# Two-layer mLSTM / sparse-attention trunk: seven block products per gate-and-up pair in both layers, with the first pair's splits in another order

## The chip, the cores and the metric

The kernel is one program on one core of a Trainium2 chip. The metric is device time in microseconds (us), the median of several executions; less is better. TensorE (PE) does the matrix products, VectorE (DVE), ScalarE (ACT) and GpSimd (POOL) the elementwise work, and SyncE (SP) issues the loads of weights.

## The reference, cut to what matters

Activations are 512 tokens by 1024 features in fp32, and the model has two layers. Each layer is a mixer (mLSTM and differential attention in layer 0, sparse attention in layer 1) and a gated feed-forward part:

```
def swiglu_ffn(h, norm_g, w_gate, w_up, w_down):
    y = rmsnorm(h, norm_g)
    return (jax.nn.silu(y @ w_gate) * (y @ w_up)) @ w_down

for layer in range(DEPTH):
    y = rmsnorm(h, mix_norms[layer])
    if layer % 2 == 0:
        h = h + mlstm_diff_mixer(y, pos, layer, *mix_params[layer])
    else:
        h = h + nsa_mixer(y, pos, *mix_params[layer])
    h = h + swiglu_ffn(h, *ffn_params[layer])
return rmsnorm(h, final_norm)
```

`w_gate` and `w_up` are 1024 x 2816, `w_down` is 2816 x 1024. The change touches `y @ w_gate` and `y @ w_up` alone.

## The kernel before, in words

**Split operands.** Every large product is made of fp32r operands in two parts, high and low: high x high, high x low, low x high, three matmuls that add up in one PSUM bank. ACT copies a weight tile to its high part (`split_high`), DVE subtracts to get the low part (`split_low`), PE multiplies.

**Units.** Weights come in units of 1024 x 128, one load each. A table (`UNIT_LIST`) numbers them through the whole program. A raw unit goes to slot number mod `RAW` (4), its split to slot number mod `SPL` (2). SP issues the load of unit u once the low split of unit u - 4 is done. Each engine runs its own instructions in the order in which they are written; semaphores alone tie the engines together.

**Gate and up stage.** It has 22 pairs (`HT`), a gate unit and an up unit each. A plain unit is 24 matmuls of 128 x 512 (`feature_unit`, 8 tiles of the inner dimension by 3). After it DVE takes the bank, times the norm's factor `rinv`, into a `work` tile (`take`); when both halves of a pair are taken and ACT has made the silu, POOL multiplies them (`product`), ACT makes the high part of the result (`ffn_high`) and DVE the low (`ffn_low`).

**Fast pairs.** `FAST` is `(1,)`: in layer 1 the first 6 pairs (`PLAIN`) are plain and the other 16 are done by `fast_quad`. The pair's weights are a 2 x 2 array of blocks (A11, A12 the halves of the gate unit, A21, A22 those of the up unit), y is another (B11 to B22: halves of the features by halves of the tokens), and seven block products stand in for eight, on sums of blocks: A11 x B11, A12 x B21, S2 x T2, S1 x T1, S3 x T3, S4 x B22, A22 x T4. Each is 12 matmuls of 128 x 256, so a pair is 84 of these where a plain pair is 48 of 128 x 512. Between them ACT copies partial results out of PSUM (`fast_copy`), and the next product into that bank waits for the copy (`part_taken`). The y blocks, scaled by `rinv` beforehand (`y_scaled`), their sums (`y_sum`) and their splits (`y_form_high`, `y_form_low`; tiles high_B, high_T, low_B, low_T) are made by DVE and ACT while the plain units run. For each pair DVE makes sums of weight blocks (`first_sums`, `second_sums`) and ACT and DVE split them: `gate_form_*` for A11 and A12, `s13_*` for S1 and S3, `s24_*` for S2 and S4 (both in the tile s_s_forms: of the program before, line 1837 and line 2546 are s13, line 1846 and line 2552 are s24), `a22_*` for A22 (tile a_high, a_low). The space of s_s_forms is that of the plain units' splits, so that the first s13 and s24 must wait for the last plain unit. The sums and T2 to T4 lie over the residual `hT` and over the constants, so ACT sends the residual to DRAM when the stage begins (`residual_spill`) and fetches it when the stage ends.

**Layer 0** does its 22 pairs plainly, from loops (`Fori`).

Of the kernel before, what the change touches and what calls it, by code (L numbers as in the profile page):

```python
# [82 lines left out]
def run(name, count, first=0):  # L83
# [9 lines left out]
UNIT_LIST = (L0_UNITS + run("WO0", 8) + run("UP0", 2 * HT) + run("DN0", 16) + L1_UNITS  # L93
             + run("WO1", 8) + run("UP1", 2 * HT) + run("DN1", 16))
# [12 lines left out]
FAST = (1,)  # L107
PLAIN = 6
NFAST = HT - PLAIN
FAST_UNITS = {AT[f"UP{layer}", c] for layer in FAST for c in range(2 * PLAIN, 2 * HT)}  # L110
FORMS = ("A11", "A12", "S2", "S1", "S3", "S4", "A22")
# [304 lines left out]
def trunk(nc, A, consts, out):  # L416
    with ExitStack() as ctx:
# [444 lines left out]
        def _(pe):  # L862
# [2313 lines left out]
```

## Time and profile before

| | us |
|---|---|
| median of 3 runs | 1317.62 (1317.62 to 1317.81) |
| the profiled execution, its own time | 1319.15 |
| its span in the trace | 1317.4 |
| PE busy | 1301.3 (99% of the span) |
| DVE busy | 782.5 (59%) |
| ACT busy | 605.6 (46%) |
| POOL busy | 195.6 (15%) |

What lies around the span is 1.75 us in the profiled execution. The granted TensorE clock was 1.00 of full speed nearly throughout. A plain unit's matmuls and a fast pair's are told apart by their width, 128x512 and 128x256.

### The profile page before, as it was taken

To read this page: it belongs to the slowest core of one execution; us is meant where nothing else is said; L and a number is where in the kernel's file an instruction comes from. 1 tells how busy PE (TensorE), PEld (TensorE's weight loads), DVE (VectorE), ACT (ScalarE), POOL (GpSimd) and SP (SyncE) were. 2 spreads that over 40 slices of the span, in tenths; PEclk is the share of its full clock that TensorE was granted. 3 is DMA by queue.
4 is the path that set the end of the run, shared out by engine and by line. 5 is a ranking of instruction groups with operands and counts; after the bars stand their busy time and mean duration, and the time that the engine had idled before them with its cause. 6 is when DMAs were issued, how large, how long until landed. Compare 5 with 4: busy or idle time off the path is not lost.

```text
span 1317.4 us, 18990 instructions
## 1 busy us (share of the span) xinstructions
PE 1301.3 (99%) x6992; PEld 1069.3 (81%) x6992; DVE 782.5 (59%) x1407; ACT 605.6 (46%) x1111; POOL 195.6 (15%) x212
## 2 busy tenths in 40 slices
PE   9999999999999999999999999999999999999997
PEld 7777788888888888888888875568887999998887
DVE  5678886543333333323599778776476788873222
ACT  4435765433333332222285457785434566652222
POOL 2003571221111110110000002112211000010100
PEclk9999999999999999999999999999999899999999
DMA  8332222323333333332244310001432333445311
GB/s 251 82 80 65 64 65 65 97 85 99 99 99 97 96 106 111 93 105 65 83 117 136 103 33 16 2 1 33 145 108 68 97 97 99 123 127 170 109 45 64
DMA packets 206728, 118.53 MB, mean 90 GB/s; under 512 B 5792, under 2 KB 203680, under 8 KB 206272
## 3 DMA queue, kind: packets, MB, share of 16 engines
q1 hardware_dynamic: 205936, 113.03, 29.8%
q10 hardware_dynamic: 304, 4.20, 0.8%
q0 software_dynamic: 416, 0.35, 0.3%
q8 instruction: 44, 0.72, 0.2%
q14 instruction: 28, 0.23, 0.1%
HBM read 113.37 MB, written 4.19 MB: 89 GB/s over the span
## 4 chain that ended last, share of the span: by engine, by line
PE 90%; DVE 3%; ACT 2%; POOL 2%; issue 2%; DMA 0%; SPq 0%; POOLq 0%; DVEq 0%; ACTq 0%
PE acc L865 17%; PE acc L867 17%; PE acc L866 17%; PE acc L1185 4%; PE acc L1187 4%; PE acc L1188 4%; PE acc L1516 3%; PE acc L878 2%; PE acc L879 2%; PE acc L882 2%; PE aux L1503 2%; PE aux L1423 2%; PE acc L919 1%; PE acc L1423 1%; PE acc L920 1%
## 5 line engine op out<-in xcount | busy, mean ns | idle before, releaser
L715 DVE TENSOR_TENSOR w_low<-raw_units,w_high 128x1024 fp32r<-128x1024 f32 (+2 forms) x152 | 200.9, 1322 | 362.0 <-ACT w_high L696 361.9
L696 ACT ACTIVATE w_high<-raw_units 128x1024 fp32r<-128x1024 f32 (+2 forms) x153 | 170.7, 1116 | 260.4 <-PE acc L867 222.4
L865 PE MATMUL acc<-y_high,w_high 128*128 128x512 f32 x616 | 244.6, 397 | 1.5 <-DVE w_low L715 1.5
L867 PE MATMUL acc<-y_high,w_low 128*128 128x512 f32 x616 | 240.3, 390 | 0.0
L866 PE MATMUL acc<-y_low,w_high 128*128 128x512 f32 x616 | 239.9, 389 | 0.0
L865 PE MATMUL acc<-ffn_high,w_high 128*128 128x512 f32 (+1 forms) x374 | 141.0, 377 | 0.0
L866 PE MATMUL acc<-ffn_low,w_high 128*128 128x512 f32 (+1 forms) x374 | 140.8, 377 | 0.0
L867 PE MATMUL acc<-ffn_high,w_low 128*128 128x512 f32 (+1 forms) x374 | 140.8, 377 | 0.0
L865 PEld LDWEIGHTS acc<-y_high,w_high 128*128 128x128 f32 x616 | 115.2, 187 | 26.9 <-DVE w_low L715 2.4
L867 PEld LDWEIGHTS acc<-y_high,w_low 128*128 128x128 f32 x616 | 115.1, 187 | 25.4
L866 PEld LDWEIGHTS acc<-y_low,w_high 128*128 128x128 f32 x616 | 115.3, 187 | 23.9 <-issue 0.5
L867 PEld LDWEIGHTS acc<-ffn_high,w_low 128*128 128x128 f32 x374 | 70.4, 188 | 13.0
L865 PEld LDWEIGHTS acc<-ffn_high,w_high 128*128 128x128 f32 x374 | 70.4, 188 | 12.8
L866 PEld LDWEIGHTS acc<-ffn_low,w_high 128*128 128x128 f32 x374 | 70.4, 188 | 12.8
L3034 POOL TENSOR_TENSOR work<-work,work 128x512 f32<-128x512 f32 x28 | 39.8, 1422 | 260.4 <-DVE work L2154 260.4
L2080 ACT ACTIVATE score<-score,neg_max 128x384 f32<-128x384 f32 (+3 forms) x128 | 68.7, 540 | 18.7 <-DVE neg_max L2898 18.5
L3020 POOL TENSOR_TENSOR work<-work,work 128x512 f32<-128x512 f32 x31 | 42.1, 1357 | 225.2 <-ACT work L1609 224.8
L1792 ACT ACTIVATE ffn_high<-work 128x512 f32 (+1 forms) x28 | 17.7, 633 | 101.0 <-POOL work L3034 101.0
L1185 PE MATMUL acc<-high_T,s_s_forms 128*128 128x256 f32 x192 | 55.7, 290 | 3.8 <-DVE s_s_forms L2552 3.8
L1187 PE MATMUL acc<-low_T,s_s_forms 128*128 128x256 f32 x192 | 55.5, 289 | 0.0
L1188 PE MATMUL acc<-high_T,s_s_forms 128*128 128x256 f32 x192 | 55.5, 289 | 0.0
L2154 DVE TENSOR_TENSOR work<-acc,rinv 128x512 f32<-128x512 f32 x64 | 43.8, 685 | 13.2 <-ACT rinv L1613 7.2
(410 smaller groups left out, 2662.3 us busy)
## 6 DMA issues: line engine op xcount, KB each, us to landing
raw_units<-in_l_w_gate_dram SPq DMA_DIRECT2D x44, 512.0 KB, 3.9
raw_units<-in_l_w_up_dram SPq DMA_DIRECT2D x44, 512.0 KB, 3.9
raw_units<-in_l_w_down_dram SPq DMA_DIRECT2D x32, 704.0 KB, 4.6
raw_units<-in_l_w_in_dram SPq DMA_DIRECT2D x43, 512.0 KB, 3.9
raw_units<-in_l_w_out_dram SPq DMA_DIRECT2D x16, 512.0 KB, 4.1
raw_units<-in_l_w_in_dram SPq DMA_DIRECT2D x10, 256.0 KB, 3.1
raw_units<-in_l_cmp_w_k_dram SPq DMA_DIRECT2D x4, 512.0 KB, 3.9
raw_units<-in_l_cmp_w_v_dram SPq DMA_DIRECT2D x4, 512.0 KB, 4.2
```

The costliest lines, as they stand in the source:

```text
L696: act.activation(dst, src, ACT.Copy).then_inc(S("split_high"), 1)
L715: dve.tensor_tensor(dst, src, high.bitcast(F32), ALU.subtract).then_inc(S("split_low"), 1)
L865: pe.matmul(o, ah, bh, start=first, stop=False)
L866: pe.matmul(o, ah, bl, start=False, stop=False)
L867: return pe.matmul(o, al, bh, start=False, stop=last)
L1185: pe.matmul(out, wh_k, y_high_of[y][:, c], start=start and k == 0, stop=False, skip_group_check=True)
L1187: pe.matmul(out, wh_k, y_low_of[y][:, c], start=False, stop=False, skip_group_check=True)
L1188: mm = pe.matmul(out, wl_k, y_high_of[y][:, c], start=False, stop=(k == KT // 2 - 1), skip_group_check=True)
L2080: act.activation(probs_at(n), probs_at(n), ACT.Exp, scale=-1.0, bias=nmx[:, n % 16:n % 16 + 1], accum_out=rsum[:, n % 16:n % 16 + 1]).then ...
L2154: return dve.tensor_tensor(dst, ps(tile)[lo:hi, cols], rinv[lo:hi, cols], ALU.mult)
L3020: pool.tensor_tensor(tmp[0][:, 0:T], tmp[0][:, 0:T], tmp[1 + m % 2][:, 0:T], ALU.add)\
L3034: pool.tensor_tensor(up, tmp[2 * (t % 2)][:, 0:T], up, ALU.mult).then_inc(S("ffn_prod"), 1)
```

## The change

`FAST` becomes `(0, 1)`: layer 0's last 16 pairs are done by seven products too, with places of their own for its y. A unit that is never loaded (`GAP0`, `GAP1`) stands ahead of the fast pairs in the numbering, so that a pair lies in an even and the next odd raw slot. The constants from `K_ROPEC` on, which layer 0's forms overwrite, are fetched again by ACT's queue behind the residual. In both layers s24 is made ahead of s13 for every pair, and PE waits for each by itself; ahead of the first fast pair ACT makes the gate form and s24, s13 before the ffn_high of the same step, DVE the sums and the gate form before it takes unit 10, and the y forms lie one step apart (T4 at step 9).

```
-FAST = (1,)
+FAST = (0, 1)
 PLAIN = 6
 NFAST = HT - PLAIN
+def up_units(layer, first):
+    gap = run(f"GAP{layer}", (first + 2 * PLAIN) % 2)
+    return run(f"UP{layer}", 2 * PLAIN) + gap + run(f"UP{layer}", 2 * NFAST, 2 * PLAIN)
...
             def load(eng, u, view, src, it=0, per=0):
+            last = u - RAW if u - RAW not in GAPS else u - 2 * RAW
+            if last in FAST_UNITS:
+                name, c = stage_of(last)
+                eng.wait_ge(S("form_low"), forms_split(int(name[2]), c // 2) + (2 if c % 2 else 4))
...
@@ fast_quad, on PE @@
-                pe.wait_ge(S("form_low"), forms_split(layer, t) + 3)
+                pe.wait_ge(S("form_low"), forms_split(layer, t) + 2)
                 pe.wait_ge(S("part_taken"), 4 * q + 1)
                 product("S2", "T2", x)
-                pe.wait_ge(S("form_low"), forms_split(layer, t) + 2)
+                pe.wait_ge(S("form_low"), forms_split(layer, t) + 3)
                 product("S1", "T1", z)
...
@@ fast_up, on ACT @@
-                hi_at = {3: ["B11"], 4: ["B21"], 5: ["T1", "B22"], 6: ["T2"], 7: ["T3"], 8: ["T4"]}
+                hi_at = {3: ["B11"], 4: ["B21"], 5: ["T1"], 6: ["B22"], 7: ["T2"], 8: ["T3"], 9: ["T4"]}
...
-                    ffn_post(layer, c // 2, c % 2)
+                    if c == 2 * PLAIN - 2:
+                        gate_form_high(layer, PLAIN)
+                    if c == 2 * PLAIN - 1:
+                        s24_high(layer, PLAIN)
+                        s13_high(layer, PLAIN)
                     for f in hi_at.get(c, ()):
                         y_form_high(layer, f)
-                    if c == 2 * PLAIN - 2:
-                        gate_form_high(layer, PLAIN)
-                s13_high(layer, PLAIN)
-                s24_high(layer, PLAIN)
+                    ffn_post(layer, c // 2, c % 2)
...
                 act.dma_start(hT, spill).then_inc(S("residual_moved"), 16)
+                if layer == 0:
+                    act.dma_start(kc[:, K_ROPEC:K_END], consts[:, K_ROPEC:K_END]).then_inc(S("consts_in"), 16)
...
@@ fast_up, on DVE @@
-                low_at = {4: ["B11"], 5: ["B21"], 6: ["T1", "B22"], 7: ["T2"], 8: ["T3", "T4"]}
+                low_at = {4: ["B11"], 5: ["B21"], 6: ["T1", "B22"], 7: ["T2"], 8: ["T3"], 9: ["T4"]}
...
+                    if c == 2 * PLAIN - 2:
+                        first_sums(layer, PLAIN)
+                        gate_form_low(layer, PLAIN)
+                        second_sums(layer, PLAIN)
                     ffn_post(layer, c // 2, c % 2)
...
-                    if c == 2 * PLAIN - 2:
-                        first_sums(layer, PLAIN)
-                        gate_form_low(layer, PLAIN)
-                        second_sums(layer, PLAIN)
+                s24_low(layer, PLAIN)
                 s13_low(layer, PLAIN)
-                s24_low(layer, PLAIN)
```

On ACT, from the split of unit 10 in layer 1 to the first copy of the first fast pair, before (w_high is a unit's split, `work_62<-work_62` a silu):

```order
L696 ACTIVATE w_high_56<-raw_units 128x1024
L1787 ACTIVATE work_60<-work_60 128x512
L1816 ACTIVATE high_T_134<-y_t_170 128x1024
L696 ACTIVATE w_high_58<-raw_units 128x1024
L1792 ACTIVATE ffn_high<-work_61 128x512
L1787 ACTIVATE work_62<-work_62 128x512
L1828 ACTIVATE gate_form_high<-raw_units 128x1024
L1792 ACTIVATE ffn_high<-work_63 128x512
L1837 ACTIVATE s_s_forms<-s_s_sums_149 128x2x512
L1846 ACTIVATE s_s_forms<-raw_units 128x2x512
L1855 ACTIVATE a_high<-raw_units 128x512
L1871 ACTIVATE work_60<-acc 128x256
```

and of the changed kernel (line 1862 is s24, line 1853 is s13), the same stretch, which stands alike in layer 0:

```order
L711 ACTIVATE w_high_58<-raw_units 128x1024
L1832 ACTIVATE high_T_133<-y_scaled_first 128x1024
L1803 ACTIVATE work_60<-work_60 128x512
L711 ACTIVATE w_high_56<-raw_units 128x1024
L1832 ACTIVATE high_T_134<-y_t_191 128x1024
L1808 ACTIVATE ffn_high<-work_61 128x512
L1844 ACTIVATE gate_form_high<-raw_units 128x1024
L1803 ACTIVATE work_62<-work_62 128x512
L1862 ACTIVATE s_s_forms<-raw_units 128x2x512
L1853 ACTIVATE s_s_forms<-s_s_sums_148 128x2x512
L1808 ACTIVATE ffn_high<-work_63 128x512
L1871 ACTIVATE a_high<-raw_units 128x512
```

The two splits into s_s_forms have moved ahead of the last plain pair's ffn_high, and s24 is the first of them; the copy of the first partial result still stands behind that ffn_high.

On DVE, from the split of unit 11 in layer 1, before:

```order
L715 TENSOR_TENSOR w_low_59<-raw_units,w_high_58 128x1024
L2154 TENSOR_TENSOR work_61<-acc,rinv 128x512
L2154 TENSOR_TENSOR work_62<-acc,rinv 128x512
L2461 TENSOR_TENSOR ffn_low<-work_61,ffn_high 128x512
L2530 TENSOR_TENSOR s_s_sums_149<-raw_units 128x2x512
L2519 TENSOR_TENSOR gate_form_low<-raw_units,gate_form_high 128x1024
L2539 TENSOR_TENSOR raw_units<-s_s_sums_149,raw_units 128x512
L2541 TENSOR_TENSOR raw_units<-raw_units 128x512
L2154 TENSOR_TENSOR work_63<-acc,rinv 128x512
L2546 TENSOR_TENSOR s_s_forms<-s_s_sums_149,s_s_forms 128x2x512
L2552 TENSOR_TENSOR s_s_forms<-raw_units,s_s_forms 128x2x512
```

and of the changed kernel:

```order
L2173 TENSOR_TENSOR work_61<-acc,rinv 128x512
L2529 TENSOR_TENSOR low_T_141<-y_t_191,high_T_134 128x1024
L2550 TENSOR_TENSOR s_s_sums_148<-raw_units 128x2x512
L2539 TENSOR_TENSOR gate_form_low<-raw_units,gate_form_high 128x1024
L2559 TENSOR_TENSOR raw_units<-s_s_sums_148,raw_units 128x512
L2561 TENSOR_TENSOR raw_units<-raw_units 128x512
L2173 TENSOR_TENSOR work_62<-acc,rinv 128x512
L2481 TENSOR_TENSOR ffn_low<-work_61,ffn_high 128x512
L2173 TENSOR_TENSOR work_63<-acc,rinv 128x512
L2572 TENSOR_TENSOR s_s_forms<-raw_units,s_s_forms 128x2x512
L2566 TENSOR_TENSOR s_s_forms<-s_s_sums_148,s_s_forms 128x2x512
```

The sums and the gate form have moved ahead of the take of unit 10 (work_62), so that they no longer stand between it and the take of unit 11 (work_63).

## Rows read from the trace of the kernel before

**Rows 1.** The page's busy times (us, share of the span, instructions), PE alone

```profile
PE 1301.3 (99%) x6992; PEld 1069.3 (81%) x6992; DVE 782.5 (59%) x1407; ACT 605.6 (46%) x1111; POOL 195.6 (15%) x212
```

**Rows 2.** The chain that ended last, shares by engine

```profile
PE 90%; DVE 3%; ACT 2%; POOL 2%; issue 2%; DMA 0%; SPq 0%; POOLq 0%; DVEq 0%; ACTq 0%
```

**Rows 3.** Busy times by stretch: layer 0, its down stage, layer 1

```profile
core 0: us, PE busy (x) PEld busy (x) DVE busy (x) ACT busy (x) POOL busy (x), PEclk, DMA share, GB/s
268.21:509.43 241.22, 241.22 (x1068) 199.53 (x1066) 95.04 (x112) 77.00 (x91) 30.46 (x24) 1.00 0.34 98
509.43:629.11 119.68, 119.68 (x530) 99.13 (x528) 36.38 (x32) 31.11 (x31) 11.34 (x9) 1.00 0.32 93
947.16:1016.43 69.27, 67.75 (x300) 55.18 (x298) 49.19 (x53) 28.13 (x34) 13.31 (x8) 1.00 0.38 115
1016.43:1033.13 16.70, 12.87 (x85) 12.67 (x84) 9.87 (x13) 7.42 (x11) 2.03 (x2) 0.80 0.23 64
1033.13:1184.33 151.20, 151.20 (x1262) 151.20 (x1261) 126.19 (x162) 92.26 (x148) 12.31 (x15) 1.00 0.40 110
```

**Rows 4.** Timeline of PE in layer 1: start, duration, idle before and its releaser

```profile
992.97 0.50 PE L865 MATMUL acc<-y_high,w_high 128*128 128x512 f32 x1 [0.26 <-DVE w_low L715]
...
1005.41 0.50 PE L865 MATMUL acc<-y_high,w_high 128*128 128x512 f32 x1 [1.25 <-DVE w_low L715]
...
1016.20 0.39 PE L867 MATMUL acc<-y_high,w_low 128*128 128x512 f32 x1
...
1019.18 0.28 PE L1188 MATMUL acc<-high_B,gate_form_low 128*128 128x256 f32 x1
1023.29 0.58 PE L1185 MATMUL acc<-high_T,s_s_forms 128*128 128x256 f32 x1 [3.83 <-DVE s_s_forms L2552]
...
1029.00 0.35 PE L1188 MATMUL acc<-high_T,s_s_forms 128*128 128x256 f32 x1
```

**Rows 5.** Timeline of ACT, around units 10 and 12, and one later pair

```profile
1001.57 0.63 ACT L1792 ACTIVATE ffn_high<-work 128x512 fp32r<-128x512 f32 x1 [5.49 <-POOL work L3034]
1002.11 1.04 ACT L1816 ACTIVATE high_T<-y_scaled_first 128x1024 fp32r<-128x1024 f32 x1
1003.06 1.04 ACT L696 ACTIVATE w_high<-raw_units 128x1024 fp32r<-128x1024 f32 x1
...
1019.27 0.63 ACT L1792 ACTIVATE ffn_high<-work 128x512 fp32r<-128x512 f32 x1 [5.12 <-POOL work L3034]
1019.80 1.04 ACT L1837 ACTIVATE s_s_forms<-s_s_sums 128x1024 fp32r<-128x1024 f32 x1
...
1021.69 0.61 ACT L1855 ACTIVATE a_high<-raw_units 128x512 fp32r<-128x512 f32 x1
1022.21 0.36 ACT L1871 ACTIVATE work<-acc 128x256 f32<-128x256 f32 x1
...
1044.85 0.38 ACT L1871 ACTIVATE work<-acc 128x256 f32<-128x256 f32 x1 [0.81 <-PE acc L1188]
```

**Rows 6.** Timeline of DVE from the take of unit 11

```profile
1017.12 0.68 DVE L2154 TENSOR_TENSOR work<-acc,rinv 128x512 f32<-128x512 f32 x1
1020.87 1.23 DVE L2546 TENSOR_TENSOR s_s_forms<-s_s_sums,s_s_forms 128x1024 fp32r<-128x1024 f32 x1 [3.08 <-ACT s_s_forms L1837]
1022.02 1.22 DVE L2552 TENSOR_TENSOR s_s_forms<-raw_units,s_s_forms 128x1024 fp32r<-128x1024 f32 x1
```

**Rows 7.** Timeline of POOL: products of the plain pairs 3 and 5

```profile
998.26 3.28 POOL L3034 TENSOR_TENSOR work<-work,work 128x512 f32<-128x512 f32 x1 [10.12 <-DVE work L2154]
...
1017.94 1.29 POOL L3034 TENSOR_TENSOR work<-work,work 128x512 f32<-128x512 f32 x1 [5.93 <-DVE work L2154]
```

**Rows 8.** DMA issues: size and median us to landing

```profile
raw_units<-in_l_w_gate_dram SPq DMA_DIRECT2D x44, 512.0 KB, 3.9
...
residual<-residual_spill ACTq DMA_DIRECT2D x1, 2048.0 KB, 9.3
...
shape_constants<-shape_consts_dram SPq DMA_DIRECT2D x1, 1480.0 KB, 10.5
```

More of the change, by code:

```diff
@@ L92 @@
             + run("VSW", 4))
-UNIT_LIST = (L0_UNITS + run("WO0", 8) + run("UP0", 2 * HT) + run("DN0", 16) + L1_UNITS
-             + run("WO1", 8) + run("UP1", 2 * HT) + run("DN1", 16))
+FAST = (0, 1)
+PLAIN = 6
+NFAST = HT - PLAIN
+def up_units(layer, first):
+    gap = run(f"GAP{layer}", (first + 2 * PLAIN) % 2)
+    return run(f"UP{layer}", 2 * PLAIN) + gap + run(f"UP{layer}", 2 * NFAST, 2 * PLAIN)
+UNIT_LIST = L0_UNITS + run("WO0", 8)
+UNIT_LIST += up_units(0, len(UNIT_LIST)) + run("DN0", 16) + L1_UNITS + run("WO1", 8)
+UNIT_LIST += up_units(1, len(UNIT_LIST)) + run("DN1", 16)
 UNITS = len(UNIT_LIST)
@@ L104, in stage_of @@
     return UNIT_LIST[u]
-FAST = (1,)
-PLAIN = 6
-NFAST = HT - PLAIN
 FAST_UNITS = {AT[f"UP{layer}", c] for layer in FAST for c in range(2 * PLAIN, 2 * HT)}
+GAPS = {u for u, (name, _) in enumerate(UNIT_LIST) if name[:3] == "GAP"}
 FORMS = ("A11", "A12", "S2", "S1", "S3", "S4", "A22")
@@ L115, in split_count @@
 def split_count(u):
-    return u + 1 - sum(f <= u for f in FAST_UNITS)
+    return u + 1 - sum(f <= u for f in FAST_UNITS | GAPS)
 def unit_count(u):
@@ L155, in loads_of @@
 def loads_of(u):
-    return 2 if stage_of(u)[0] == "VSW" else 1
+    return 0 if u in GAPS else 2 if stage_of(u)[0] == "VSW" else 1
 def loads_in_slot(u):
@@ L534, in trunk @@
                             .rearrange("p (f w) -> p f w", f=2)[:, :, 0:T])
-        plain_y = {3: ([row(f"y3_high{m}", 28 + m, 1, F32R) for m in range(KT)],
+        plain_y = {1: ([row(f"y1_high{m}", 8 + m, 1, F32R) for m in range(KT)],
+                       [row(f"y1_low{m}", 28 + m, 1, F32R) for m in range(KT)]),
+                   3: ([row(f"y3_high{m}", 28 + m, 1, F32R) for m in range(KT)],
                        [row(f"y3_low{m}", r, 1, F32R) for m, r in enumerate((36, 37, 38, 39, 40, 41, 6, 7))])}
-        scaled = {3: [row("y3_scaled_first", 8, 4), row("y3_scaled_last", 12, 4)]}
-        t_raw = {3: {"T1": row("y3_t1", 16, 2), "T2": row("y3_t2", 18, 2), "T4": row("y3_t4", 16, 2)}}
+        scaled = {1: [row("y1_scaled_first", 16, 4), row("y1_scaled_last", 36, 4)],
+                  3: [row("y3_scaled_first", 8, 4), row("y3_scaled_last", 12, 4)]}
+        t_raw = {1: {"T1": row("y1_t1", 40, 2), "T2": row("y1_t2", 6, 2), "T4": row("y1_t4", 40, 2)},
+                 3: {"T1": row("y3_t1", 16, 2), "T2": row("y3_t2", 18, 2), "T4": row("y3_t4", 16, 2)}}
         qraw = row("q_raw", 0, 8)
@@ L811, in load_ffn @@
                         w = (w_gate if c % 2 == (c >= 2 * PLAIN) else w_up)[layer]
-                        tile = raw[(u0 + c) % RAW][:, 0:KT * P].rearrange("p (k n) -> p k n", n=P)
-                        load(sp, u0 + c, tile, w[:, :, col(c // 2)])
+                        u = AT[f"UP{layer}", c]
+                        tile = raw[u % RAW][:, 0:KT * P].rearrange("p (k n) -> p k n", n=P)
+                        load(sp, u, tile, w[:, :, col(c // 2)])
                 else:
@@ L2248, in scaled_angles @@
             def scaled_angles(layer):
+                dve.wait_ge(S("consts_in"), 16 + 16 * layer)
                 dve.tensor_tensor(rcos[layer], ropec, rinv, ALU.mult).then_inc(S("angles"), 1)
@@ L2527, in first_sums @@
                 if t > PLAIN:
-                    dve.wait_ge(S("form_low"), forms_split(layer, t - 1) + 2)
+                    dve.wait_ge(S("form_low"), forms_split(layer, t - 1) + 3)
                 a21 = raw_of(layer, t)[0][:, 0:T]
@@ L2543, in s13_low @@
             def s13_low(layer, t):
-                dve.wait_ge(S("form_high"), forms_split(layer, t) + 2)
+                dve.wait_ge(S("form_high"), forms_split(layer, t) + 3)
                 dve.tensor_tensor(s13[:, :, T:2 * T], sums13[raw_pair(layer, t)], s13[:, :, 0:T].bitcast(F32), ALU.subtract)\
@@ L2549, in s24_low @@
             def s24_low(layer, t):
-                dve.wait_ge(S("form_high"), forms_split(layer, t) + 3)
+                dve.wait_ge(S("form_high"), forms_split(layer, t) + 2)
                 dve.tensor_tensor(s24[:, :, 1, :], raw_of(layer, t)[1][:, 0:2 * T].rearrange("p (f n) -> p f n", n=T),
```

17 lines of the change are left out of this document (7 added, 10 removed).

## The prediction

> **What bounds the kernel now.** I read the page's busy times first: PE is busy 99% of the span, DVE, at 59%, is next [rows 1]. The chain of waits agrees: 90% of it is PE's own work [rows 2]. So time goes where PE's matmuls go, and where PE stands still. The busy times by stretch then give the lengths of the stages that the change touches [rows 3]. The reader is to see three things there. Layer 0's gate and up stage, all plain, lasts 241.22 us and PE is busy in all of it. Layer 1's is three stretches, 69.27 + 16.70 + 151.20 = 237.17 us, and PE is idle in the first two. And the second, which is one fast pair alone, has a mean granted clock of 0.80 where all others have 1.00. PE's timeline names the idle places: 0.26 and 1.25 us ahead of plain units 8 and 10, both ended by a low split of DVE, and 3.83 us inside the first fast pair, ended by the low split of s24 [rows 4].
>
> **A pair by the one way and by the other.** The down stage between the layers has 528 matmuls of 128x512 in 119.68 us, 0.2267 us each; a plain pair has 48 of them, 10.88 us. The 15 fast pairs after the first take 151.20 us, 10.08 us a pair, or 0.120 us for each of 84 matmuls [rows 3]. Half the columns cost 53% of the time, so of the eighth that the algebra saves 0.80 us a pair is left. For 16 pairs that is 12.80 us.
>
> Layer 0 can run its fast pairs at layer 1's pace if DVE, ACT and POOL do the same work there. In the 151.20 us they are busy 126.19, 92.26 and 12.31 us [rows 3], so DVE fills 83% and keeps up, and the instruction order in the two layers is the same. I take 10.08 us a pair. Layer 0's first 12 units took 241.22 - 16 x 10.88 = 67.14 us without a stall. In the changed kernel DVE and ACT also make the y forms during them, as they do in layer 1, which costs nothing as long as the splits of the units stay ahead.
>
> **Units 8 and 10.** In layer 1 they did not stay ahead. ACT waited until 1001.57 us for POOL's product, made ffn_high, then the form of T3, and only at 1003.06 the high split of unit 10, for which PE stood idle until 1005.41 [rows 4, 5]. The change puts y forms ahead of that ffn_high, into a time in which ACT waits anyway (5.49 us idle before it), and leaves one form in each step. The split moves up by the 0.95 us between 1002.11 and 1003.06, and what precedes it, takes and products of steps 5 to 7, moves up as well, since two forms stood at step 5. I take both stalls as gone in layer 1 and absent in layer 0, and 0.3 us (1.25 - 0.95) in each layer as the other bound. Layer 1's first stretch without its 1.51 us of idleness and the slow start behind each is about 67.3 us; I use that for both layers.
>
> **The entry to the fast pairs.** Before, from 1016.43 to 1033.13 us, it cost 16.70 - 10.08 = 6.62 us more than a later pair [rows 3]. Its parts: PE's next matmul was due at 1019.18 + 0.12 = 1019.30 and came at 1023.29, 3.99 us late; the 27 matmuls from there to 1029.00 took 0.211 us each, not 0.120, which is 2.47 us [rows 4]. That is the lower of the clock's two levels, 1.2 GHz for 2.4, entered in the idle time, and it makes the mean of 0.80 [rows 3]. The Trainium skill (TensorE: Matmul & The Clock Gate, HAM oscillation) says the same of idle gaps; the trace agrees, and shows too that 1.25 us of idleness left the clock alone.
>
> PE was late because ACT made s13 and s24 only after the ffn_high of pair 5 at 1019.27, which had waited 5.12 us for POOL, and DVE subtracted s13 first [rows 5, 6]. Now s24 and s13 wait for unit 11 alone. Its last matmul starts at 1016.20 and ends at 1016.59 [rows 4]. ACT's s24 runs to about 1017.7, DVE's low part (1.22 us) to about 1018.95; s13's low part follows by about 1020.1. S2 is due at 1019.30 and S1 1.44 us (12 x 0.12) after S2. So the splits no longer hold PE.
>
> What is late next is the copy of the first partial result. S2 adds to the bank of A11, and waits until ACT has copied it; ACT reaches the copy behind the ffn_high of pair 5 and the a22 form. This chain starts with the take of unit 11, which DVE could only begin at 1017.12 [rows 6] and now begins at about 1016.65. Take 0.68, POOL 1.29 with 0.13 ahead of it [rows 7], then 0.53 us on ACT for ffn_high to the next start, 0.52 for a22 and 0.36 for the copy [rows 5], with 0.05 for each change of engine: 1016.65 + 0.68 + 0.13 + 1.29 + 0.05 + 0.53 + 0.52 + 0.36 + 0.05 = 1020.26. PE is then 0.96 us late. I take 1.0 us for the entry in each layer, with the clock left at 1.00. Bounds: 0 below (A11's copy in time, nothing shorter), and above by the slowest product in these rows, 3.28 us for 1.29 [rows 7], which makes 3.0 us.
>
> **POOL's product.** The row at 998.26 shows 3.28 us and that at 1017.94 1.29 us for the same instruction on tiles of the same size [rows 7]. At 1017.94 DVE was idle; at the new place s24's low split starts some 0.2 us after the product. The Trainium skill (GPSIMD Engine Reference, Specifications) says that GpSimd shares its SBUF interfaces with VectorE and is held up by VectorE instructions with two SBUF inputs, which the split is. The trace has both outcomes. By the slow one 2.0 us more is lost in a layer, by the fast one nothing; since the product begins first here, I go by the fast row.
>
> **The order s24, s13 in every later pair.** s24 waits for the S4 product, so ACT's two forms end about 1 us later than before, and the a22 form and the copy of A11 stand behind them. The copy at 1044.85 came after 0.81 us of idleness, and the a22 form before it had waited too [rows 5], so about that much cover is left: cost nothing.
>
> **Loads and transfers.** With the gap unit, raw units 12 and 13 wait for the low splits of units 9 and 10, one later than before. Unit 10's was done by 1005.4 in layer 1 [rows 4]; a load lands 3.9 us after its issue [rows 8], at 1009.3, and DVE turns to it only behind the split of unit 11, the take of unit 9 and the last y form (0.7 and 1.2 us). Cost nothing. At layer 0's end ACT's queue fetches the residual (9.3 us) and behind it the constants (10.5 us for 1480 KB) [rows 8]. The first residual add comes two units of the down stage later, 66 x 0.2267 = 14.96 us. Should the two transfers share evenly and the residual land after 19.8 us, DVE is 4.8 us late, with the split of a unit behind it that PE wants at 29.9 us. Cost nothing; without that cover up to 4.8 us. The spill at the start is layer 1's, where PE did not wait for it.
>
> **The sum.** Each layer's stage should last 67.3 + 16 x 10.08 + 1.0 = 229.6 us. Layer 0: 241.2 - 229.6 = 11.6. Layer 1: 237.2 - 229.6 = 7.6. Together 19.2 us. The profiled execution took 1319.15 us, 1.75 more than its span of 1317.4, and would take 1299.9; the median of the runs shown is 1.53 us below it, 1317.62, and gives 1298.4.
>
> **Rivals.**
> - *Slow product at the entry.* In one or both layers the product takes 3.28 us: 1300.4 or 1302.4. PE would then be idle for 3 us, between the 1.25 that left the clock and the 3.83 that did not; if the clock falls, 2.47 us more each, up to 1307.3. For: the row at 998.26. Against: it is one row, and there DVE's work had begun first.
> - *The new order doesn't help, and layer 0 is as layer 1 was.* Both stages last 237.17 us, only 4.05 us are won: 1313.6. Against: by the instruction orders the splits do stand ahead of the waiting ffn_high.
> - *The transfers at layer 0's end delay its down stage* by up to 4.8 us: 1303.2.
> - *Slower than before:* the new order lengthens every fast pair. If ACT's and DVE's work on s13 behind s24 comes to PE's path, a pair grows by one DVE split, 1.15 us (1020.87 to 1022.02 [rows 6]), in 32 pairs 36.8 us, and the time is 1335.2. It decides from 19.2 / 32 = 0.60 us a pair. Against: S1 follows S2 by 1.44 us, which covers the 1.15, and 0.81 us of cover stands ahead of the copy.
>
> **How the numbers follow.** The forecast, both stages at about 229.6 us with the entries between 0 and 2 us, has 0.71, and its own range is 1296.4 to 1300.5. The slow product has 0.16, the order without effect 0.05, the transfers 0.05, slower 0.03. The range reaches from both entries at nothing, 1296.4, to both products slow and something over, 1303.5. What a measurement here can tell from no change is about 0.2%, 2.6 us; all cases but the last lie beyond it on the fast side, and I leave 0.01 for no difference.
>
> **What would show it.** In the profile after: fast pairs of 10.08 us in layer 0; layer 0's gate and up stage near 229.6 us and layer 1's the same; no idle time ahead of units 8 and 10; ahead of s_s_forms' first matmul in each layer about 1 us of idle time, released by ACT's copy and not by a low split; the clock at 1.00 through both. The prediction is wrong if a POOL product of 2 us or more stands at an entry, if the stage of layer 0 has waits on splits that layer 1 lacks, or if later pairs are longer than 10.08 us.

## The result, and the profile after

The changed kernel takes 1299.34 us (median of four, 1298.77 to 1299.89), the kernel before beside it 1317.71 (1317.62 to 1318.48): a ratio of 0.9859, 95% interval 0.9842 to 0.9876. It is faster by 18.4 us or 1.4%, where 1298.4 us had been forecast. The profiled execution took 1298.77 us, 1.77 more than its span.

The page of the changed kernel: busy times, chain, and the group of the matmuls on s_s_forms (the last column is the idle time just before them and what ended it).

```profile
span 1297.0 us, 20009 instructions
PE 1285.3 (99%) x7568; PEld 1084.0 (84%) x7568; DVE 868.4 (67%) x1522; ACT 654.4 (50%) x1214; POOL 203.9 (16%) x212
PE 88%; DVE 6%; issue 2%; ACT 2%; POOL 2%; DMA 0%; SPq 0%; POOLq 0%; DVEq 0%; ACTq 0%
L1201 PE MATMUL acc<-high_T,s_s_forms 128*128 128x256 f32 x384 | 108.8, 283 | 2.0 <-DVE s_s_forms L2572 2.0
```

PE is still the bound, at 99%; DVE went from 59% to 67% [rows 1]. The only idle time at the fast pairs is 2.0 us in all, ahead of s_s_forms.

Busy times by stretch of the changed kernel: layer 0's first 12 units, its first fast pair, the 15 others, the down stage; then layer 1's three. They answer to [rows 3].

```profile
core 0: us, PE busy (x) PEld busy (x) DVE busy (x) ACT busy (x) POOL busy (x), PEclk, DMA share, GB/s
267.30:334.45 67.15, 67.15 (x299) 55.34 (x298) 49.31 (x54) 27.97 (x34) 15.30 (x8) 1.00 0.40 119
334.45:345.73 11.28, 10.29 (x86) 10.11 (x84) 9.24 (x11) 7.15 (x12) 2.51 (x2) 1.00 0.27 77
345.73:496.93 151.20, 151.20 (x1263) 151.20 (x1261) 124.64 (x163) 91.56 (x149) 16.14 (x15) 1.00 0.40 110
496.93:616.64 119.71, 119.71 (x531) 99.14 (x529) 36.45 (x33) 31.52 (x32) 10.05 (x8) 1.00 0.42 127
934.67:1001.81 67.14, 67.14 (x300) 55.34 (x298) 49.30 (x54) 27.96 (x34) 15.28 (x8) 1.00 0.39 119
1001.81:1013.10 11.29, 10.29 (x85) 10.11 (x84) 9.25 (x11) 7.16 (x12) 2.51 (x2) 1.00 0.27 77
1013.10:1164.30 151.20, 151.20 (x1262) 151.20 (x1261) 124.64 (x163) 91.55 (x149) 16.15 (x15) 1.00 0.40 110
```

The two layers' stages are now alike: 229.62 us for 241.22 in layer 0, 229.63 for 237.17 in layer 1, so 11.6 and 7.5 us are won. PE is busy through the first 12 units (the stalls at units 8 and 10 are gone), later pairs take 10.08 us in both layers, the clock is 1.00, and the down stage behind layer 0 has its old length (119.71 for 119.68). The spans differ by 20.4 us, 1.3 more than the stages; of this 0.9 lies ahead of layer 0's stage, which begins at 267.31 for 268.21. That place moves from kernel to kernel (268.14 in e1 and e2, 267.36 in e3, 270.13 in e9); what moves it was not looked for.

The first fast pair costs 1.2 us more than a later one, 0.99 of it idle. Its entry in layer 1, engine by engine (start, duration, idle time before it and what ended it): PE, ACT, DVE, POOL.

```profile
1004.56 0.28 PE L1204 MATMUL acc<-high_B,gate_form_low 128*128 128x256 f32 x1
1005.84 0.36 PE L1201 MATMUL acc<-high_T,s_s_forms 128*128 128x256 f32 x1 [1.00 <-DVE s_s_forms L2572]
...
1001.68 0.63 ACT L1803 ACTIVATE work<-work 128x512 f32<-128x512 f32 x1 [3.42 <-DVE work L2173]
1002.21 1.04 ACT L1862 ACTIVATE s_s_forms<-raw_units 128x1024 fp32r<-128x1024 f32 x1
1003.16 1.04 ACT L1853 ACTIVATE s_s_forms<-s_s_sums 128x1024 fp32r<-128x1024 f32 x1
1004.32 0.63 ACT L1808 ACTIVATE ffn_high<-work 128x512 fp32r<-128x512 f32 x1
1004.86 0.61 ACT L1871 ACTIVATE a_high<-raw_units 128x512 fp32r<-128x512 f32 x1
1005.38 0.36 ACT L1887 ACTIVATE work<-acc 128x256 f32<-128x256 f32 x1
...
1001.56 0.68 DVE L2481 TENSOR_TENSOR ffn_low<-work,ffn_high 128x512 fp32r<-128x512 f32 x1
1002.16 0.69 DVE L2173 TENSOR_TENSOR work<-acc,rinv 128x512 f32<-128x512 f32 x1
1003.29 2.08 DVE L2572 TENSOR_TENSOR s_s_forms<-raw_units,s_s_forms 128x1024 fp32r<-128x1024 f32 x1 [0.45 <-ACT s_s_forms L1862]
1005.29 1.21 DVE L2566 TENSOR_TENSOR s_s_forms<-s_s_sums,s_s_forms 128x1024 fp32r<-128x1024 f32 x1
...
1002.99 1.30 POOL L3054 TENSOR_TENSOR work<-work,work 128x512 f32<-128x512 f32 x1 [6.34 <-DVE work L2173]
```

The matmul at 1005.84 waits for two things, DVE's low split of s24 and ACT's copy of the first partial result. The trace names the low split of s24, but that ends at 1003.29 + 2.08 = 1005.37; ACT's copy ends at 1005.38 + 0.36 = 1005.74, 0.10 before PE starts. By these rows the copy held PE, as forecast, and the low split is only 0.37 us behind it as a second cause, because it took 2.08 us and not the 1.22 of [rows 6]. That has to be shown.

### The profile page after: what moved, and what is told of

It is laid out like the page before. It is cut to its first block, busy times and chain, and to the rows that moved or that the text cites. A ratio compares the mean times of both kernels' runs of the same rounds, so it can differ in the third digit from the quotient of the medians.

```text
span 1297.0 us, 20009 instructions
## 1 busy us (share of the span) xinstructions
PE 1285.3 (99%) x7568; PEld 1084.0 (84%) x7568; DVE 868.4 (67%) x1522; ACT 654.4 (50%) x1214; POOL 203.9 (16%) x212
## 4 chain that ended last, share of the span: by engine, by line
PE 88%; DVE 6%; issue 2%; ACT 2%; POOL 2%; DMA 0%; SPq 0%; POOLq 0%; DVEq 0%; ACTq 0%
PE acc L881 12%; PE acc L883 11%; PE acc L882 11%; PE acc L1201 8%; PE acc L1203 8%; PE acc L1204 8%; PE acc L1532 3%; PE acc L894 2%; PE acc L895 2%; PE acc L898 2%; PE aux L1519 2%; PE aux L1439 2%; POOL work L3054 2%; DVE w_low L730 1%; PE acc L935 1%
## 5 line engine op out<-in xcount | busy, mean ns | idle before, releaser
L730 DVE TENSOR_TENSOR w_low<-raw_units,w_high 128x1024 fp32r<-128x1024 f32 (+1 forms) x120 | 161.7, 1347 | 233.2 <-ACT w_high L711 233.1
L881 PE MATMUL acc<-y_high,w_high 128*128 128x512 f32 (+1 forms) x360 | 144.8, 402 | 0.0
L883 PE MATMUL acc<-y_high,w_low 128*128 128x512 f32 (+1 forms) x360 | 140.7, 391 | 0.0
L882 PE MATMUL acc<-y_low,w_high 128*128 128x512 f32 (+1 forms) x360 | 140.3, 390 | 0.0
L1201 PE MATMUL acc<-high_T,s_s_forms 128*128 128x256 f32 x384 | 108.8, 283 | 2.0 <-DVE s_s_forms L2572 2.0
L1204 PE MATMUL acc<-high_T,s_s_forms 128*128 128x256 f32 x384 | 108.7, 283 | 0.0
L1203 PE MATMUL acc<-low_T,s_s_forms 128*128 128x256 f32 x384 | 108.7, 283 | 0.0
L883 PEld LDWEIGHTS acc<-y_high,w_low 128*128 128x128 f32 (+1 forms) x360 | 67.0, 186 | 15.3
L881 PEld LDWEIGHTS acc<-y_high,w_high 128*128 128x128 f32 (+1 forms) x360 | 67.2, 187 | 14.5 <-issue 0.8
L882 PEld LDWEIGHTS acc<-y_low,w_high 128*128 128x128 f32 (+1 forms) x360 | 67.2, 187 | 14.1 <-issue 0.5
L2099 ACT ACTIVATE score<-score,neg_max 128x384 f32<-128x384 f32 (+3 forms) x128 | 68.7, 541 | 18.7 <-DVE neg_max L2918 18.5
L1201 PEld LDWEIGHTS acc<-high_T,s_s_forms 128*128 128x128 f32 x384 | 73.7, 192 | 2.3 <-DVE s_s_forms L2572 2.3
```

The lines of the kernel that those rows point to most:

```text
L730: dve.tensor_tensor(dst, src, high.bitcast(F32), ALU.subtract).then_inc(S("split_low"), 1)
L881: pe.matmul(o, ah, bh, start=first, stop=False)
L882: pe.matmul(o, ah, bl, start=False, stop=False)
L883: return pe.matmul(o, al, bh, start=False, stop=last)
L1201: pe.matmul(out, wh_k, y_high_of[y][:, c], start=start and k == 0, stop=False, skip_group_check=True)
L1203: pe.matmul(out, wh_k, y_low_of[y][:, c], start=False, stop=False, skip_group_check=True)
```

## The experiments

Theory A, the prediction's: the pairs give 0.80 us each, the order of the splits decides the entry, and what is left there is ACT's copy behind ffn_high and a22. Rival B: the low split of s24, as the trace says. Each kernel was timed beside the kernel before on the same chip (medians there: 1318.51 us for e1 to e4, 1317.12 for e5 to e8, 1317.81 for e9 to e12). What tells kernels apart best is the length of the first fast pair, a later one being 10.08:

| | change | us | ratio (95%) | first fast pair, layer 0 / 1 |
|---|---|---|---|---|
| e1 | both layers, old order | 1313.58 | 0.9964 (0.9951 to 0.9977) | 16.35 / 15.64 |
| e2 | layer 1 alone, new order | 1311.31 | 0.9941 (0.9925 to 0.9958) | none / 11.29 |
| e3 | y forms behind ffn_high | 1308.72 | 0.9923 (0.9906 to 0.9940) | 14.16 / 12.63 |
| e4 | copy first | 1298.45 | 0.9844 (0.9828 to 0.9861) | 10.77 / 10.76 |
| e5 | product on DVE | 1298.67 | 0.9859 (0.9842 to 0.9875) | 11.07 / 10.87 |
| e6 | both of these | 1297.36 | 0.9848 (0.9832 to 0.9865) | 10.15 / 10.15 |
| e7 | e6 with 5 plain pairs | 1303.44 | 0.9895 (0.9879 to 0.9912) | 14.02 / 12.54 |
| e8 | s13 first again | 1300.68 | 0.9874 (0.9858 to 0.9891) | 11.91 / 11.91 |
| e9 | 5 plain, all products on DVE | 1303.34 | 0.9887 (0.9871 to 0.9904) | 13.90 / 12.49 |
| e10 | 6 plain, all products on DVE | 1297.17 | 0.9845 (0.9828 to 0.9861) | 10.17 / 10.15 |
| e11 | the changed kernel again | 1299.28 | 0.9864 (0.9847 to 0.9880) | 11.17 / 11.28 |
| e12 | e6 again | 1297.43 | 0.9851 (0.9834 to 0.9867) | 10.17 / 10.17 |

### e1: seven products in both layers, everything in the old order

Against the changed kernel:

```
-                hi_at = {3: ["B11"], 4: ["B21"], 5: ["T1"], 6: ["B22"], 7: ["T2"], 8: ["T3"], 9: ["T4"]}
+                hi_at = {3: ["B11"], 4: ["B21"], 5: ["T1", "B22"], 6: ["T2"], 7: ["T3"], 8: ["T4"]}
...
-                    if c == 2 * PLAIN - 1:
-                        s24_high(layer, PLAIN)
-                        s13_high(layer, PLAIN)
+                    ffn_post(layer, c // 2, c % 2)
...
+                s13_high(layer, PLAIN)
+                s24_high(layer, PLAIN)
```

and the same on DVE (sums and gate form behind the take of unit 10), with s13 ahead of s24 in all pairs and the waits to match.

> Seven products in both layers, but with the order of before throughout: s13 ahead of s24, both behind the last plain pair's ffn_high, y forms behind ffn_post, two forms at step 5, sums and gate form behind the take of unit 10. My theory: layer 0's gate and up stage becomes a copy of layer 1's of before, 237.2 us for 241.2, with the 3.8 us of idle time, the clock at half for some 7 us behind it and the idle time ahead of units 8 and 10; layer 1's stays 237.2; the time is 1317.7 - 4.0 = 1313.7 us. Rival: the order counts for little and the seven products bring most of the gain: both stages near 230 to 233 us, under 1308 us.

Measured: 1313.58 us. In layer 0, the first fast pair by stretch and its first matmul on s_s_forms with the next two:

```profile
336.25:352.61 16.36, 12.54 (x86) 12.33 (x85) 9.88 (x13) 7.42 (x11) 2.02 (x2) 0.79 0.24 65
...
343.11 0.58 PE L1201 MATMUL acc<-high_T,s_s_forms 128*128 128x256 f32 x1 [3.82 <-DVE s_s_forms L2571]
343.48 0.42 PE L1203 MATMUL acc<-low_T,s_s_forms 128*128 128x256 f32 x1
343.70 0.42 PE L1204 MATMUL acc<-high_T,s_s_forms 128*128 128x256 f32 x1
```

The old entry, with its 3.82 us of idleness and its half clock (0.21 us from matmul to matmul), now stands in both layers. Layer 0's stage is 235.67 us; of the 11.6 us that it gives with the new order only 5.55 come. On its chip e1 is 4.9 us faster than before, where the whole change gives 18.4: without the order most of the gain is missing. Layer 1's stage was 234.95 and not 237.17, though the order there is that of before: 0.13 us idle ahead of unit 10 for 1.25, and a shorter stretch at half clock. For unit 10 the traces show the reason. The product of pair 3, for which ACT waits before it splits unit 10, took 2.14 us here and 3.28 before [rows 7]:

```profile
992.60 2.14 POOL L3053 TENSOR_TENSOR work<-work,work 128x512 f32<-128x512 f32 x1 [10.12 <-DVE work L2172]
```

PE begins unit 10 at 998.61, 3.87 us after that product's end, and before at 1005.41, 3.87 after its end as well. In this order the product's length passes to PE. Why the half clock lasted less long was not tried. The profiled execution was e1's fastest, 2.65 us below its median, so these lengths are rather short ones.

### e2: the new order, seven products in layer 1 alone

```
-FAST = (0, 1)
+FAST = (1,)
```

with layer 0's units numbered without a gap and its constants not fetched twice.

> The new order and the gap unit in layer 1 alone; layer 0 plain, as before. My theory: layer 1's stage goes from 237.2 to 229.6 us, layer 0's stays 241.2, the time is 1317.7 - 7.6 = 1310.1 us, and the two parts (the seven products in layer 0 behind the new order, 11.6 us, and this one) add up to the whole 18.4 to 19.2 us. Rival: the parts do not add up, since something in layer 0's change helps or hurts layer 1: more than 1 us off 1310.1.

Measured: 1311.31 us, 7.2 below before on this chip. Layer 0's stage is 241.22 us as before, layer 1's 229.63 for 237.17: 7.54 us for the new order with its gap unit, where 7.6 had been forecast (e1, which has the gap unit and the old order, was not slower in this layer than before). The rest of the gain, 11.6 us of stage, is layer 0's.

### e3: the y forms behind ffn_high

```
-                hi_at = {3: ["B11"], 4: ["B21"], 5: ["T1"], 6: ["B22"], 7: ["T2"], 8: ["T3"], 9: ["T4"]}
+                hi_at = {3: ["B11"], 4: ["B21"], 5: ["T1", "B22"], 6: ["T2"], 7: ["T3"], 8: ["T4"]}
...
+                    ffn_post(layer, c // 2, c % 2)
                     for f in hi_at.get(c, ()):
                         y_form_high(layer, f)
-                    ffn_post(layer, c // 2, c % 2)
```

> The changed kernel with one thing undone: ACT makes the y forms behind the ffn_high or silu of each step again, with T1 and B22 both at step 5. My theory: the idle time ahead of units 8 and 10 comes back in both layers, 1.5 us of idleness and a slow start each, 1.8 us a layer; the entry to the fast pairs stays at 1.2 us; the time is 1299.3 + 3.6 = 1302.9 us. Rival: those stalls went with something else (the place of the gate form or the loads), and the time stays 1299.3.

Measured: 1308.72 us, 5.8 over what was expected. The stalls at units 8 and 10 came back: 1.39 and 1.25 us in layer 1, 1.39 and 0.12 in layer 0, where the product of pair 3 took 2.14 us and not 3.28. But the entry did not stay at 1.2 us. PE's idle places in layer 1 (units 8 and 10, the entry), then DVE and ACT between:

```profile
986.66 0.50 PE L881 MATMUL acc<-y_high,w_high 128*128 128x512 f32 x1 [1.39 <-DVE w_low L730]
999.11 0.50 PE L881 MATMUL acc<-y_high,w_high 128*128 128x512 f32 x1 [1.25 <-DVE w_low L730]
...
1015.53 0.36 PE L1201 MATMUL acc<-high_T,s_s_forms 128*128 128x256 f32 x1 [2.33 <-DVE s_s_forms L2572]
...
1002.25 1.23 DVE L730 TENSOR_TENSOR w_low<-raw_units,w_high 128x1024 fp32r<-128x1024 f32 x1 [0.86 <-ACT w_high L711]
1003.39 0.68 DVE L2173 TENSOR_TENSOR work<-acc,rinv 128x512 f32<-128x512 f32 x1
...
1006.39 0.64 ACT L1808 ACTIVATE ffn_high<-work 128x512 fp32r<-128x512 f32 x1 [4.17 <-POOL work L3054]
...
1011.87 0.68 DVE L2173 TENSOR_TENSOR work<-acc,rinv 128x512 f32<-128x512 f32 x1
```

A late split of unit 11 delays the take of unit 9 queued behind it (1003.39), this the product and ffn_high of pair 4, this the gate form, and DVE then reaches the take of unit 11 at 1011.87, 1.70 us after the first fast pair begins (1010.17), where the changed kernel has it 0.35 after. The entry is idle for 1.35 more: 2.33 us in layer 1, and 2.38 in layer 0, where the clock fell too. So the place of the forms is worth 5.0 and 4.6 us of stage (234.61 and 234.26 us for 229.6), not some 1.8 each. What DVE's queue hands on to the entry is the late split of unit 11 (ACT made its high part only behind a y form) and not PE's stall: in layer 0, where PE stood for 0.12 us at unit 10, the entry was idle as long as in layer 1.

### e4, e5, e6: the copy first, the product on DVE, both

e4, on ACT:

```
                     for f in hi_at.get(c, ()):
                         y_form_high(layer, f)
+                    if c == 2 * PLAIN - 1:
+                        fast_copy(layer, PLAIN, "A11")
                     ffn_post(layer, c // 2, c % 2)
```

e5, on DVE, with POOL's product of that pair left out:

```
                     ffn_post(layer, c // 2, c % 2)
+                    if c == 2 * PLAIN - 1:
...
+                        dve.tensor_tensor(up, tmp[2 * (t % 2)][:, 0:T], up, ALU.mult).then_inc(S("ffn_prod"), 1)
```

> The changed kernel with ACT's copy of the first fast pair's A11 result put ahead of the last plain pair's ffn_high and of the a22 form. Theory A, the copy holds PE (it ended 0.10 us before PE went on, s24's low split 0.47 us before): the entry shrinks by about 0.4 us in each layer, to where the low split is ready, 1298.5 us. Theory B, the low split of s24 holds PE, as the profile's releaser says: nothing changes, 1299.3 us. In the profile, the idle time ahead of the first matmul on s_s_forms goes from 1.00 to about 0.58 us by A and stays 1.00 by B.

> The changed kernel with the last plain pair's product (silu times up) made by DVE ahead of s24's low split, and not by POOL. It tests two things: that the low split took 2.08 us because POOL's product ran beside it (then it takes 1.22 us here), and what holds PE. The low split then ends some 0.6 us earlier, the copy only some 0.2 us earlier, since ACT's s13 form stands ahead of ffn_high. By theory A (copy) the entry shrinks by 0.2 us a layer, 1298.9 us; by theory B (low split) by 0.6 us a layer, 1298.1 us. If POOL is not the reason for 2.08 us, the low split stays at 2.08.

> Both: the copy first and the product on DVE. By theory A with POOL as the reason for the slow low split, nothing holds PE any more than 0.1 to 0.2 us: the idle time of 1.00 us in each layer goes, 1299.3 - 2.0 = 1297.3 us. By theory B it is 1298.1 us as with the product on DVE alone.

e4, layer 0: PE's first matmul on s_s_forms, ACT's copy, DVE's low split of s24.

```profile
338.25 0.38 PE L1201 MATMUL acc<-high_T,s_s_forms 128*128 128x256 f32 x1 [0.45 <-DVE s_s_forms L2575]
...
336.89 0.36 ACT L1887 ACTIVATE work<-acc 128x256 f32<-128x256 f32 x1
...
336.07 2.13 DVE L2575 TENSOR_TENSOR s_s_forms<-raw_units,s_s_forms 128x1024 fp32r<-128x1024 f32 x1 [0.40 <-ACT s_s_forms L1862]
```

With the copy done by 337.25 PE starts 0.54 us earlier than in the changed kernel, now directly behind the low split (338.20). The low split itself ends only 0.1 us earlier than there, counted from the pair's start (3.43 us for 3.55), and PE now begins 0.05 us behind it, where it began 0.47 behind it in the changed kernel. Had the low split been what held PE, no more than that 0.1 would have been won. That is A.

e5, layer 0: the same, with DVE's product.

```profile
338.83 0.36 PE L1201 MATMUL acc<-high_T,s_s_forms 128*128 128x256 f32 x1 [0.77 <-issue]
...
338.38 0.36 ACT L1887 ACTIVATE work<-acc 128x256 f32<-128x256 f32 x1
...
336.16 0.69 DVE L2623 TENSOR_TENSOR work<-work,work 128x512 f32<-128x512 f32 x1
336.77 1.22 DVE L2572 TENSOR_TENSOR s_s_forms<-raw_units,s_s_forms 128x1024 fp32r<-128x1024 f32 x1
```

Without POOL's product beside it the low split takes 1.22 us again and is done at 337.99, 0.84 before PE starts; the copy, done at 338.74, is what PE waits for. So POOL's product is what made the low split slow, and the copy still sets the entry, a little earlier (0.77 and 0.58 us idle). DVE multiplies in 0.69 us where POOL takes 1.30, so that the product ends 0.66 us sooner after the pair's start, but ffn_high then stands behind s13 on ACT and begins only 0.2 sooner.

e6, layer 0: first fast pair by stretch.

```profile
335.37:345.52 10.15, 10.15 (x85) 10.11 (x84) 9.11 (x11) 6.31 (x11) 0.88 (x1) 1.00 0.26 75
```

No idle time is left. Both causes taken away give 1297.36 us (1297.3 expected). Of the 1.13 us by which the first pair shrinks, the copy alone gives about half (e4) and the product alone 0.2 to 0.4 (e5).

### e8: s13 ahead of s24 again

```
                     if c == 2 * PLAIN - 1:
-                        s24_high(layer, PLAIN)
                         s13_high(layer, PLAIN)
+                        s24_high(layer, PLAIN)
```

and the same in every pair, on DVE, and in PE's and the loads' waits.

> The changed kernel with s13 ahead of s24 again in every fast pair, all else as changed. The low split of s24 is then the second one and ends about 1.1 us later; at the entry it is ready at about 0.7 us behind where PE went on. My theory: 0.7 us more in each layer, 1300.7 us, and the later pairs stay at 10.08 us. Rival: the order counts in no pair, 1299.3 us.

Measured: 1300.68 us. In layer 0, PE's entry and the two low splits:

```profile
339.54 0.39 PE L1201 MATMUL acc<-high_T,s_s_forms 128*128 128x256 f32 x1 [1.57 <-DVE s_s_forms L2572]
...
336.22 2.12 DVE L2566 TENSOR_TENSOR s_s_forms<-s_s_sums,s_s_forms 128x1024 fp32r<-128x1024 f32 x1 [0.40 <-ACT s_s_forms L1853]
338.27 1.21 DVE L2572 TENSOR_TENSOR s_s_forms<-raw_units,s_s_forms 128x1024 fp32r<-128x1024 f32 x1
```

Here the low split of s24 is the cause: it ends at 339.48. The order among the two is worth 0.6 us at each entry and nothing in the later pairs, 10.08 us either way. With both behind ffn_high as well (e1) the first pair took 15.64 and 16.35 us, for 11.91 here: which of the two comes first is the small part of the change's order. That their place ahead of ffn_high is the large part is not shown by itself, since e1 also takes back the place of the y forms, which alone makes the pair 12.63 and 14.16 us (e3), and the order on DVE.

### e7, e9, e10: fewer plain pairs, and all plain products on DVE

A further pair done by seven products would save 0.8 us a layer. e7 is e6 with `PLAIN = 5` and the y forms closer together; e9 moves all plain products to DVE in it; e10 does that with six plain pairs.

```
-PLAIN = 6
+PLAIN = 5
...
-                hi_at = {3: ["B11"], 4: ["B21"], 5: ["T1"], 6: ["B22"], 7: ["T2"], 8: ["T3"], 9: ["T4"]}
+                hi_at = {3: ["B11"], 4: ["B21"], 5: ["T1", "B22"], 6: ["T2"], 7: ["T3", "T4"]}
```

> As the one before, with 5 plain pairs for 6 in each layer, so 17 fast ones; the y forms stand one or two to a step, all before step 8. A fast pair is 0.80 us shorter than a plain one: 1.6 us less than with both edits, 1295.7 us, if the denser y forms stay hidden. Rival: two forms at steps 5 and 7 delay the splits of units 8 and 9 and the stalls of 0.3 to 1.3 us come back in both layers, which takes the gain away: 1296.5 to 1299.

> Five plain pairs as before, copy first, and DVE makes the product of every plain pair. The run with five plain pairs lost 0.86 and 2.1 us of idle time in each layer, with the gate form and s24 late on DVE. If DVE is simply full there (by the sum of its rows from unit 1 to unit 9 some 44 us of work in 43.5 us), taking the product from POOL ends the doubled DVE instructions (about 1.1 us each) and ACT's waits for POOL, but adds 0.6 us of work a pair: s24 still comes about 1.4 us late, 1298.5 us. If POOL was the whole reason, no idle time is left: 1295.8 us.

> Six plain pairs, copy first, DVE makes the product of every plain pair. With six plain pairs nothing was late any more with the last product alone on DVE, so that taking the others can bring nothing: 1297.4 us. Should DVE be near full here too, its added 3 us a layer come to light as idle time of PE of up to 1 us a layer: 1299.4 us.

e7 and e9 are slower than e6 by 6.1 and, against e12 on its chip, 5.9 us, where a gain or a loss of under 2 us was expected: all these expectations missed. e9: PE's entries of layer 0 and 1, a stretch of layer 0 behind it, and DVE's low split of s24 with what stands ahead of it.

```profile
331.58 0.58 PE L1201 MATMUL acc<-high_T,s_s_forms 128*128 128x256 f32 x1 [2.11 <-DVE s_s_forms L2575]
1000.71 0.39 PE L1201 MATMUL acc<-high_T,s_s_forms 128*128 128x256 f32 x1 [2.12 <-DVE s_s_forms L2575]
...
331.40:334.80 3.40, 3.22 (x15) 3.22 (x16) 3.40 (x5) 2.07 (x4) 0.00 (x0) 0.50 0.00 0
...
328.92 0.68 DVE L2176 TENSOR_TENSOR work<-acc,rinv 128x512 f32<-128x512 f32 x1
329.69 0.69 DVE L2627 TENSOR_TENSOR work<-work,work 128x512 f32<-128x512 f32 x1
330.30 1.22 DVE L2575 TENSOR_TENSOR s_s_forms<-raw_units,s_s_forms 128x1024 fp32r<-128x1024 f32 x1
```

Of e9's time 2.2 us lie ahead of layer 0's stage in the profiled execution (it begins at 270.13 for 267.96 in e10); its two stages are 4.5 us longer than e10's. DVE works without a gap of note from 316.86 to 330.30 and reaches the low split so late that PE stands for 2.11 us; in layer 0 the clock halves behind it, which makes that first pair 1.4 us longer than layer 1's. e7 has the same wait (2.10 us) and 0.86 ahead of the gate form besides. The y forms need as much of DVE in five pairs as in six: DVE is the limit at the entry, though over the whole changed program it is busy 67%. Taking the products from POOL (e9) does away with the 0.86 us ahead of the gate form and makes the two stages 2.2 us shorter than e7's, but leaves the 2.11, so for that wait POOL was not the reason. Three of the forms stand at one step, and DVE has three gaps of 0.56 to 0.74 us between 305 and 317 us; another placing of the forms was not tried. e10, with six, has no such wait and equals e6.

### e11, e12: the changed kernel and e6 on one chip

> The changed kernel as it is, once more, beside the next one on the same chip. 1299.3 us.

> The kernel with the copy first and the last product on DVE, once more, beside the changed kernel: 2.0 us less than that by theory A, 1297.3 us.

e11 gave 1299.28 us (1298.88 to 1300.78), e12 1297.43 (1297.23 to 1298.96), e10 1297.17 (1296.89 to 1297.41). The changed kernel with the copy first and no POOL product beside the low split is faster by 1.9 to 2.1 us, what its spans say as well (1295.5 and 1295.4 for 1297.5).

## Why the prediction was right

- **The pairs.** 10.08 us in layer 0 too, 0.80 a pair: exact. DVE's 124.64 us in 151.20 left room, as read from layer 1.
- **Units 8 and 10.** Gone in both layers, the first 12 units at 67.14 us. The step took 67.3; e3 puts the forms back and has the stalls back. What the step did not see is that these stalls follow POOL's product in the old order: behind one of 3.27 or 3.28 us they are 1.39 (unit 8) and 1.25 us (unit 10), behind one of 2.13 or 2.14 us some 0.25 and 0.12 us (before, e1, e3). In the changed kernel the products of pairs 2 and 3 took 3.27 us in both layers, and PE did not stand.
- **The entry.** Forecast 1.0 us, measured 1.20 above a later pair. That the stage came out at 229.62 for 229.6 is in part luck: the units took 0.16 less than the 67.3 forecast, the entry 0.2 more. The chain take, product, ffn_high, a22, copy is the right one: counted from PE's due time (1004.56 + 0.12 = 1004.68) it gave 0.96 us, and was 1.16. Its links were as long as forecast; but the take began at 1002.16, 0.35 us into the pair for a forecast 0.22, because DVE's ffn_low of pair 4 (1001.56, 0.68 us) stands ahead of it, and PE started 0.10 behind the copy for 0.05. It held PE, by e4.
- **The releaser in the profile** would be the copy, the prediction said. This sign came out wrong: the profile names the low split, though e4 and e5 show that the copy held PE. Their ends lie 0.37 us apart, for the reason in the next point.
- **POOL's product.** Fast, 1.30 us, as taken. The step's "by the fast one nothing" was right for PE by luck: the delay went to DVE's low split (2.08 for 1.22), which stayed 0.37 us short of mattering. In e4 it did matter. The forecast also counted one slow row; the trace of before has two products of 1.67 us and one of 2.13 beside it in layer 1's plain pairs, where DVE makes the y forms, and none over 1.30 in layer 0's, so the risk lay nearer than "it is one row" says.
- **The order s24, s13.** Free in later pairs, as said, and worth 0.6 us at an entry (e8).
- **Loads, transfers.** No trace of them: down stage 119.71 us. At layer 0's end the residual landed after 10.5 us and the constants after 13.8.
- **The clock.** 1.00 through both stages; what e1 brings back, half clock, is what the new order avoids.
- **The sum.** Forecast 19.2 us, stages 19.1. The median came 0.9 above 1298.4. The forecast took its sum off an execution 1.53 us over its median, and set that 1.53 against the changed kernel too; there the profiled execution was 0.57 below the median. Between medians the gain is 18.4 and 18.5 us (e11), somewhat under the stages' 19.1; that rest is as small as the differences among executions of one kernel, and stays open.

The rivals fell: no slow product at an entry (1.30 us in both layers), order effective (e1 is the kernel of the rival "order doesn't help", forecast there at 1313.6 and measured at 1313.58, though with stages somewhat shorter than the 237.17 us it was made of), no lengthened pair. The chances given add up to 1.01.

## What to carry to other kernels

When an instruction in order waits long for another engine, put everything that is ready or needed sooner ahead of it; here undoing that order alone gave back 13 to 14 of 18 us (e1), which takes back all parts of the order at once. A split made late at one unit came back, through the queue of one engine, as 1.3 to 2.9 us at the next change of stage (e3). Where an instruction waits for two things, compare the end times of both with its start before believing the releaser that the profile names. An engine at 67% over a program can still be full in the ten microseconds that decide.

## What the runs showed of the hardware

**POOL and DVE did not run side by side.** In the changed kernel, POOL's products of pairs 3 and 4 in layer 1 and DVE's instructions around them:

```profile
984.13 3.28 POOL L3054 TENSOR_TENSOR work<-work,work 128x512 f32<-128x512 f32 x1 [8.23 <-DVE work L2173]
994.51 2.14 POOL L3054 TENSOR_TENSOR work<-work,work 128x512 f32<-128x512 f32 x1 [7.09 <-DVE work L2173]
...
983.91 1.22 DVE L2522 SCALAR_TENSOR_TENSOR y_t<-y_t,y_scaled_last 128x1024 f32<-128x1024 f32 x1
985.04 1.22 DVE L2529 TENSOR_TENSOR low_T<-y_t,high_T 128x1024 fp32r<-128x1024 f32 x1
...
994.28 1.22 DVE L2529 TENSOR_TENSOR low_T<-y_t,high_T 128x1024 fp32r<-128x1024 f32 x1
995.41 2.31 DVE L2550 TENSOR_TENSOR s_s_sums<-raw_units 128x1024 f32<-128x1024 f32 x1
```

At 984.13 DVE's two instructions ran at full speed and POOL ended at 987.41, 1.15 us after the second. At 994.51 it ended at 996.65, 1.15 after DVE's first, and DVE's second, 1.22 alone, ended 1.07 after POOL. At the entry POOL began first, ran in 1.30, and DVE's split ended 1.08 after it. So each time one waited for the other, and the waiting shows as a long instruction. It is not always the one that began second that waits: DVE's instruction at 985.04 began after POOL's and was not held up. In e9 and e10, where POOL makes no product of a plain pair in the two stages, no DVE instruction of 128x1024 there takes over 1.23 us; in the changed kernel two in each layer take 2.08 to 2.32. (In e10 the DVE instruction of 128x512 beside POOL's work on the later fast pairs takes 1.11 to 1.16 us, where it takes 0.69 in the changed kernel.) The Trainium skill (GPSIMD Engine Reference, Specifications) lists contention between GpSimd and VectorE instructions with two SBUF inputs; the trace agrees and shows it both ways, POOL held up by DVE (3.28 us for 1.30) and DVE by POOL (2.31 for 1.22). Why POOL waited for two DVE instructions once and for one the other time is open.

**The clock after 2 us of idleness went either way.** In the profiled executions, idle times up to 1.57 us (e8) never moved it. 2.10 to 2.38 us (e3, e7, e9) brought it to 1.2 GHz in layer 0 each time, and 2.11 to 2.33 us in layer 1 of the same kernels never. 3.82 us did it in both layers of e1, for 6.8 us in layer 0 and 3.4 in layer 1. These are one execution of each kernel. Layer 0 may not fall every time: e7's profiled execution took 1304.29 us at a mean granted clock of 0.998, the three others 1305.36, 1302.58 and 1302.52 at 0.997, 0.999 and 0.999. What differs ahead of the two places was not tried.
